# Attention scores and column sums as fp32r products of split operands, in the second block

## The reference

```python
h = rmsnorm(x, attn_norm[l])
sb_q, sb_k, sb_v, df_q, df_k, df_v = split(h @ w_in[l])        # 512 columns each
# stick-breaking attention, 8 heads of 64
z = q @ k.T * scale                                            # strict causal
w = exp(log_sigmoid(z) + sum of log_sigmoid(-z) over later keys)
sb_out = w @ v
# differential attention, 4 heads with 2 maps of 64, values of 128; q and k through rope
p = softmax(where(allowed, q @ k.T * scale, neg))              # for each map
df_out = rmsnorm((p[0] - lam * p[1]) @ v, subln_norm[l]) * (1 - lambda_init)
x = x + concat(sb_out, df_out) @ w_o[l]
h = rmsnorm(x, mlp_norm[l])
x = x + square(relu(h @ w_ff1[l])) @ w_ff2[l]                  # 4096 hidden
```

## Time and profile before

| | |
|---|---|
| median of 3 runs | 1955.8 us (1955.64 to 1956.62) |
| profiled execution, its own time | 1955.69 us |
| its span | 1953.9 us |
| mean granted TensorE clock | 0.999 of full |
| TensorE busy | 98% of the span |
| VectorE, ScalarE, GpSimd busy | 47%, 43%, 45% |

### The profile page before, as it was taken

One profiled execution on the slowest core, in us unless ns is written; L12 is line 12 of the kernel. 1 busy time (PEld: TensorE's weight loads), 2 busy tenths in 40 slices (PEclk: granted clock), 3 DMA queues, 4 the chain that ended last, 5 costly groups with the idle time before them and its releaser, 6 DMA issues. The chain is left out here.

```text
span 1953.9 us, 25592 instructions
## 1 busy us (share of the span) xinstructions
PE 1923.8 (98%) x9150; PEld 1510.5 (77%) x9150; DVE 916.7 (47%) x1420; ACT 834.5 (43%) x1269; POOL 881.6 (45%) x1188
## 2 busy tenths in 40 slices
PE   9999999999999999999999999999999999999998
PEld 7866766788888887777688888887777688888887
DVE  5487877432241346777541313133777643222132
ACT  4466555543242345555532223134555542222233
POOL 4322221456456465343355455454443355454543
PEclk9999999999999999999999999999999999999999
DMA  8211111233234233222134233333222223243322
GB/s 234 65 44 44 34 44 33 87 106 110 84 89 119 76 96 99 75 66 75 48 107 116 78 108 97 87 97 95 78 66 76 65 85 110 86 119 86 109 86 76
DMA packets 318100, 168.77 MB, mean 86 GB/s; under 512 B 15028, under 2 KB 313367, under 8 KB 317847
## 3 DMA queue, kind: packets, MB, share of 16 engines
q1 hardware_dynamic: 314432, 162.38, 28.9%
q10 hardware_dynamic: 3542, 4.76, 1.0%
HBM read 160.29 MB, written 2.10 MB: 83 GB/s over the span
## 5 line engine op out<-in xcount | busy, mean ns | idle before, releaser
L737 POOL TENSOR_TENSOR wlo<-raw,whi 128x256 fp32r<-128x256 f32 x1164 | 865.2, 775 | 1042.2 <-ACT whi L778 1042.2
L1621 PE MATMUL accs<-Xh,whi 128*128 128x512 f32 x1448 | 581.3, 401 | 0.1
L1623 PE MATMUL accs<-Xh,wlo 128*128 128x512 f32 x1448 | 565.1, 390 | 0.0
L1622 PE MATMUL accs<-Xl,whi 128*128 128x512 f32 x1448 | 563.9, 389 | 0.0
L778 ACT ACTIVATE whi<-raw 128x1024 fp32r<-128x1024 f32 x291 | 307.7, 1061 | 267.6 <-PE accs L1623 218.5
L1621 PEld LDWEIGHTS accs<-Xh,whi 128*128 128x128 f32 x1448 | 272.1, 188 | 58.6 <-issue 3.7
L1623 PEld LDWEIGHTS accs<-Xh,wlo 128*128 128x128 f32 x1448 | 271.8, 188 | 58.4
L1622 PEld LDWEIGHTS accs<-Xl,whi 128*128 128x128 f32 x1448 | 272.4, 188 | 56.1 <-issue 3.6
L1621 PE MATMUL accs<-Uh,whi 128*128 128x512 f32 x744 | 289.7, 389 | 0.8 <-DVE xT L1210 0.8
L1622 PE MATMUL accs<-Ul,whi 128*128 128x512 f32 x744 | 289.4, 389 | 0.0
L1623 PE MATMUL accs<-Uh,wlo 128*128 128x512 f32 x744 | 289.4, 389 | 0.0
(11 more groups left out here) (303 smaller groups left out, 1913.8 us busy)
## 6 DMA issues: line engine op xcount, KB each, us to landing
raw<-in_w_ff_dram SPq DMA_DIRECT2D x128, 512.0 KB
raw<-in_w_in_dram SPq DMA_DIRECT2D x71, 512.0 KB
raw<-in_w_gate_up_dram SPq DMA_DIRECT2D x44, 512.0 KB
raw<-in_w_down_dram SPq DMA_DIRECT2D x16, 512.0 KB
raw<-in_w_o_dram SPq DMA_DIRECT2D x16, 512.0 KB
px<-W ACTq DMA_DIRECT2D x64, 64.0 KB, 2.0
raw<-in_w_down_dram SPq DMA_DIRECT2D x8, 384.0 KB
W<-in_x_dram SPq DMA_DIRECT2D x4, 512.0 KB, 6.1
```

Source lines behind the costliest of these rows:

```text
L737: pool.tensor_tensor(lo[:, ks], raw[:, unit_no % RAW, ks], hi[:, ks].bitcast(F32), ALU.subtract).then_inc(sems["wlo"], 1)
L1621: mmul(y, whi[:, slot, k], xh[:, k], start=(i == 0), stop=False)
L1622: mmul(y, whi[:, slot, k], xl[:, k], start=False, stop=False)
L1623: last = mmul(y, wlo[:, slot, k], xh[:, k], start=False, stop=(i == len(ks) - 1))
```

## The change

Scores: the queries and keys of the second block get split as the weights do. ScalarE writes the rounded value into a free column tile of `Uh`, GpSimd the rest into `Ul`, at the items `sbq`, `sbk` and `rope`; for `rope` only with `j` < 3. The score product becomes three fp32r products for each head, for `qb` > 0. Column sums: `ssq` (new item `ssplit`, ScalarE and VectorE, at the end of the `prep` items) and the squares of `dv` (ScalarE squares `O` twice, GpSimd subtracts) are split too, and the sum is two fp32r products with a matrix of ones; the factor 1/1024 or 1/128 moves into ScalarE's logarithm. The order of the other items stays as it is.

```diff
+SB_Q, SB_K, DF_Q, DF_K = 3, 7, 2, 6
-    return s
+    return s + [("ssplit",)]                      # outputs(); also behind the last ffn_round of a layer
...
+                elif item[0] == "dv":             # GpSimd
+                    c = 4 + item[1]
+                    pool.wait_ge(sems["O_act"], at("O_act", 1))
+                    pool.tensor_tensor(Ul[:, c], sq[:, :], Uh[:, c].bitcast(F32), ALU.subtract).then_inc(sems["s_lo"], 1)
+                elif item[0] in ("sbq", "sbk", "rope"):
+                    split = qk_split(item)
+                    if split:
+                        src, c = split
+                        pool.wait_ge(sems["qk_hi"], at("qk_hi", 1))
+                        pool.tensor_tensor(Ul[:, c], src, Uh[:, c].bitcast(F32), ALU.subtract).then_inc(sems["qk_lo"], 1)
...
+                elif kind == "ssplit":            # ScalarE
+                    act.wait_ge(sems["sq"], at("sq"))
+                    act.wait_ge(sems["xl"], at("xl"))
+                    A(Uh[:, 0], ssq[:, :], ACT.Copy).then_inc(sems["s_hi"], 1)
...
+                    A(Uh[:, 4 + item[1]], O[:, :], ACT.Square).then_inc(sems["s_hi"], 1)    # dv, ahead of the square into sq
...
+                elif kind in ("sbq", "sbk"):
+                    src, c = qk_split(item)
+                    act.wait_ge(sems["acc"], at("acc", 1))
+                    A(Uh[:, c], src, ACT.Copy).then_inc(sems["qk_hi"], 1)
+                    act.wait_ge(sems["qk_hi"], at("qk_hi", 1))
+                elif kind == "rope" and qk_split(item):
+                    src, c = qk_split(item)
+                    act.wait_ge(sems["rp"], at("rp", 1))
+                    A(Uh[:, c], src, ACT.Copy).then_inc(sems["qk_hi"], 1)
+                    act.wait_ge(sems["qk_hi"], at("qk_hi", 1))
...
+                elif kind == "ssplit":            # VectorE
+                    dve.wait_ge(sems["s_hi"], at("s_hi", 1))
+                    TTn(Ul[:, 0], ssq[:, :], Uh[:, 0].bitcast(F32), ALU.subtract).then_inc(sems["s_lo"], 1)
...
+            def scores(bank, q, k, qb):           # TensorE
+                n = P * (qb + 1)
+                for a, b in ((Uh, Uh), (Ul, Uh), (Uh, Ul)):
+                    for h in range(2):
+                        mmul(bank[:, h, 0:n], a[hrows(h), q, P * qb:n], b[hrows(h), k, 0:n], start=(a is Uh and b is Uh), stop=False)
+            def column_sums(c):
+                pe.wait_ge(sems["ones_r"], 1)
+                pe.wait_ge(sems["s_lo"], at("s_lo"))
+                mmul(M[:, :], ones_r[:, :], Uh[:, c], start=True, stop=False)
+                return mmul(M[:, :], ones_r[:, :], Ul[:, c], start=False, stop=True)
...
-                    mmul(M[:, :], o1024, ssq[:, :], start=True, stop=True).then_inc(sems["M_fill"], 1)
+                    column_sums(0).then_inc(sems["M_fill"], 1)
...
-                    mmul(M[:, :], o128, sq[:, :], start=True, stop=True).then_inc(sems["M_fill"], 1)
+                    column_sums(4 + item[1]).then_inc(sems["M_fill"], 1)
...
-                    for h in range(2):
-                        mmul(S[:, h, 0:n], sbq[hrows(h), P * qb:n], sbk[hrows(h), 0:n], start=True, stop=False)
+                    if qb:
+                        pe.wait_ge(sems["qk_lo"], at("sb_split"))
+                        scores(S, SB_Q, SB_K, qb)
...
+                    if qb and item[1] < 3:        # d1
+                        pe.wait_ge(sems["qk_lo"], at("df_split"))
+                        scores(TT, DF_Q, DF_K, qb)
```

More of the change, by code:

```diff
@@ L133 @@
     "lay": dict(),
-    "sbq": dict(acc=1), "sbk": dict(acc=1),
+    "sbq": dict(acc=1, qk_hi=1, qk_lo=1), "sbk": dict(acc=1, qk_hi=1, qk_lo=1),
     "dfr": dict(acc=1, swap=1), "rope": dict(rp=1),
@@ L149, in events_of @@
         return dict(S_fill=1, S_act=1)
+    if kind == "rope" and item[2] < 3:
+        return dict(rp=1, qk_hi=1, qk_lo=1)
     if kind == "hn1" and item[1] == 3:
@@ L189, in marks_of @@
     if kind == "dv":
-        return dict(at_read="O_fill", o_sq="O_act")
+        return dict(at_read="O_fill")
     if kind == "on1":
@@ L398, in ffn_round @@
                 out.append(("prep", c, ("vec", R_AN + c)))
-        return out
+        return out + ([("ssplit",)] if last else [])
     s += [("rotary",)] + ffn_round(8, 0, False) + ffn_round(8, 1, False) + ffn_round(6, 2, True)
@@ L607, in build, with qk_split @@
         ssc, scb, scr = nsm[:, 0:8], nsm[:, 8:12], nsm[:, 12:16]
+        def qk_split(item):
+            if item[0] == "sbq":
+                return sbq, SB_Q
+            if item[0] == "sbk":
+                return sbk, SB_K
+            return ((dfk, DF_K) if item[1] else (dfq, DF_Q)) if item[2] < 3 else None
         def pt_view(at, qb):
@@ L1822, in stage @@
                     pe.wait_ge(sems["S_dve"], at("S_dve"))
-                    for h in range(2):
-                        mmul(S[:, h, 0:n], sbq[hrows(h), P * qb:n], sbk[hrows(h), 0:n], start=True, stop=False)
+                    if qb:
+                        pe.wait_ge(sems["qk_lo"], at("sb_split"))
+                        scores(S, SB_Q, SB_K, qb)
+                    else:
+                        for h in range(2):
+                            mmul(S[:, h, 0:n], sbq[hrows(h), P * qb:n], sbk[hrows(h), 0:n], start=True, stop=False)
                     for h in range(2):
@@ L1852, in stage @@
                     pe.wait_ge(sems["T_dve"], at("T_dve"))
-                    for m in range(2):
-                        mmul(TT[:, m, 0:n], dfq[hrows(m), P * qb:n], dfk[hrows(m), 0:n], start=True, stop=False)
+                    if qb and item[1] < 3:
+                        pe.wait_ge(sems["qk_lo"], at("df_split"))
+                        scores(TT, DF_Q, DF_K, qb)
+                    else:
+                        for m in range(2):
+                            mmul(TT[:, m, 0:n], dfq[hrows(m), P * qb:n], dfk[hrows(m), 0:n], start=True, stop=False)
                     for m in range(2):
```

38 lines of the change are left out of this document (27 added, 11 removed).

## The result

The changed kernel takes 2059.22 us (median, 2057.94 to 2059.82) against 1956.21 us (1955.64 to 1958.23) of the kernel before beside it: ratio 1.0524, 95% interval 1.0506 to 1.0542, 103.0 us slower. The forecast was slower, 2041 us, with a range of 2004 to 2065. The profiled execution took 2058.95 us (span 2057.1), the one before 1955.69 (span 1953.9).

A forecast was written before the change was run, and what follows sets the result against it. TensorE, busy 98% of the span, was taken as the bound. 1955.7 + 76.4 of waits - 6.7 of savings outside the stops = 2025.4; with 15.4 for the clock, 2041 us, range 2004 to 2065.

The forecast's parts named there:

- Rival 5: GpSimd is not held at its subtractions, so the products' 11.1 us are the whole result: 1944.6 us; chance 0.03.
- rival 1: TensorE's clock stays up or is back at once after the stops: 2025 us; chance 0.15.
- The forecast's 76.4: Delay from TensorE's new waits in both layers, 38.2 us each: 10.0 + 11.3 + 11.3 + 3.85 + 1.75.
- The second steady stop: Steady period, rope 1 ahead of the next mmA sq: TensorE stops for some 6.5 us.
- the first period: At j = 0, rope's subtractions delay TensorE: 5.0 us at the first stop, 10.0 us in all.
- The sign that I had named: TensorE's first product of mmA dv and mmA sq waits for GpSimd's wlo 4 to 7 us, three periods per layer.
- Rival 2: The second stop doesn't inherit the first; steady period costs 6.0 instead of 11.3 us: 2000, with some clock 2005; chance 0.09.
- rival 3: The two heads' fp32r score products don't overlap; each set costs +0.96 instead of -0.42 us: 2054 us; chance 0.05.
- rival 4: Each fp32r score round pays its weight load; the counted sets give +1.9 instead of -3.9 us: 2047 us; chance 0.05.
- 15.4 us forecast: Clock loss of TensorE behind its stops, taken as 1.1 us each; upper bound 2.8 each, 39 in all.
- the 14: Forecast stops of TensorE over both layers: four of 4.6, four of 5.0, two of 5.1, four of 6.5 us.
- the other insertions: Remaining inserted splits stay hidden in the steady period; at a layer's start they cost under 1 us, left to the range.

The follow-up runs named there:

- Experiment 1: The changed kernel with GpSimd's subtractions issued behind the quarters of the next two units (last dv of a layer: one): 1989.27 us, ratio 1.0170.
- experiment 8: Kernel 7 with all splits of queries and keys made, but the scores taken as float32 products: 1966.51 us, ratio 1.0050.
- experiment 2: The changed kernel with spare, unread products on TensorE in front of the places where it will stop: 2035.64 us, ratio 1.0406.
- Experiment 12: Kernel 7 with every GpSimd subtraction in the second block cut into four of 128 columns: 1956.59 us, ratio 1.0001.
- kernel 7: Kernel 6 with dv and on1 of each layer's last pair as in the kernel before: 1960.82 us, ratio 1.0022.
- 10: Kernel before plus only split column sums, dv's subtraction behind one unit, last pair as before, float32 scores: 1953.57 us, ratio 0.9987.
- kernel 9: Kernel before with only the five norms' column sums made as two fp32r products: 1955.10 us, ratio 0.9996.
- kernel 6: Kernel 5 with ScalarE's copy for rope moved behind the whi of the next mmA: 1964.96 us, ratio 1.0044.
- kernel 5: Kernel 1 with GpSimd's subtraction of dv behind the quarters of one unit instead of two: 1980.88 us, ratio 1.0123.

## Why the prediction was right, and where it was not

**The mechanism** was right: GpSimd and ScalarE walk the list in order, a subtraction that waits for a result of the moment takes away the lead of two units, and TensorE stops at `mmA dv`, at the next `mmA sq`, at the first early unit and at the last `on1`. Experiment 1 shows it directly: the same work in another place leaves no stop for quarters. Rival 5 (GpSimd not held) fell with GpSimd's waits of 133.9 and 106.8 us, rival 1 (the clock stays up) with the 16 low stretches.

**The stops** came to 68.2 us by the rows. The forecast's 76.4 is the delay that they cause, with what the items between them save already taken off: 68.2 less 4.3 (11 saved in all, 6.7 counted apart), so 63.9, is to be laid beside it. The chain from the rotated result to the two quarters measured 853.49 - 850.00 = 3.49 us against 3.75, since the subtraction took 1.27 us where I took 1.5. The second steady stop was 6.30 against 6.5. The first was 3.43 against 4.6: the result was there at 833.04, as TensorE finished the masks, and not 0.9 us behind, since TensorE was itself late by small waits. In the first period the stops were 4.23 and 3.41 us where I had 10.0 in all; in the last, 4.70 (forecast 5.1) and 2.10 (2.15). The sign that I had named, waits of 4 to 7 us for quarters in three periods, came as 3.3 to 6.3.

```profile
774.93 0.80 PE L1691 MATMUL accs<-Xh,whi 128*128 128x512 f32 x1 [4.23 <-POOL wlo L751]
...
979.73 0.47 PE L1716 MATMUL accs<-Uh,whi 128*128 128x512 f32 x1 [4.70 <-issue]
```

**Rival 2** (the second stop doesn't inherit the first) is refuted: ScalarE's swap DMAs went out behind `dv`'s squares at 844.61, VectorE's multiplication followed 3.97 us later (forecast 3.93), and the time is 54 us above that rival's 2005.

**The products** were nearly right: 5.2 us for the scores by the rows of their items against 5.9, a set 0.37 where I took 0.42, and a sum 0.36 to 0.45 cheaper against 0.40. That experiment 8 came to 5.7 is in part luck, since the clock has a share in it. Rivals 3 (heads don't overlap) and 4 (each round pays its load) are refuted too: by rival 3 a set would have cost 0.96 more, and the rule behind rival 4 isn't borne out, since rounds on the same rows follow each other 0.22 us apart.

**The clock** was the term that was mis-sized: 15.4 us forecast, 35 by the rows and some 24 by experiment 2. I took 1.1 us for each stop, because "the stops are not so long that each must meet a fall"; but each of the changed kernel's did, also the two of 2.1 us at the last `on1`, which I had not counted among the 14. TensorE worked at the low level for 3.2 to 6.8 us behind each, of which half is lost: 2.2 us for each of 16 stretches. The upper bound that I had set, 39, was nearer. The Trainium skill (TensorE: Matmul & The Clock Gate, "HAM oscillation") has a kernel that loses the clock in every wait between two bursts of products; the changed kernel's trace agrees, with 16 of 16. Other kernels here don't: see the last section.

**Not foreseen** were the small waits: 7.1 us of scores and 5.5 us of transposes waiting for VectorE. I had put "under 1 us" on the other insertions. Experiment 12 shows a reason for the wait at `d3` in kernel 7: GpSimd's longer instruction holds VectorE's. In the changed kernel itself no such instruction lies beside `d2` in these six places; there both operations of `d2` fall beside quarters (0.72 and 0.71 us, before 0.72 and 0.35), which is less than half of the 0.9 us that each transpose waits. The rest of it, and the waits of the scores, no run explains. What kept kernel 7 above before are the scores' splits: in its order they cost about 12 us (8 against 10), some 2 of it by the clock, about twice what their products save.

So 2041 missed 2059 by 18 us: 12.5 too many for the stops, 19.6 too few for the clock, 9.3 for small waits that had no term (77.5 - 68.2), and 1.7 that the rows don't place. That the miss is no larger is in part luck: the errors have opposite signs.

**Open.** All changed kernels, the one with only the norms' sums included, reach the end of the first units 0.6 us later than before and the end of the 17th to 28th 0.9 us later, in a stretch where the change adds only one copy of 0.23 us on VectorE, for the matrix of ones (at 69.8 us in kernel 9). The step at the 17th is a longer wait of TensorE for VectorE's scaling of the values (1.05 us at 163.7 in kernel 9, 0.73 before). It takes nearly half of the 2.0 us that the norms' sums save, and no run tells why. What the scores' splits cost beyond the 4 us that kernel 12 gave back was not taken apart further.

## What to carry to other kernels

Where engines walk one list in order, a new instruction costs by what is queued behind it: place it behind the work that feeds others, on each engine of its chain (GpSimd, then ScalarE here: 70 us and 16 us without taking away any work). Before an engine with idle time gets the work of a busy one, look at what it makes ahead of time, and at whose instructions it will hold. A stop of TensorE can be dearer than its length: allow for a half-speed stretch behind it, here 35 us on 68.

## What the runs showed of the hardware

- In the changed kernel a stop of TensorE of 2.10 us (1005.50 to 1007.60) had a granted clock of 0.50 behind it, while the stop of 1.1 us and those of 1.0 to 1.4 us in kernel 7 left it at full.

```profile
1005.60:1007.50 1.90, 0.00 (x0) 0.00 (x0) 0.00 (x0) 0.52 (x1) 1.31 (x2) 1.00 0.00 0
1007.60:1011.00 3.40, 3.40 (x8) 2.73 (x9) 0.67 (x1) 1.32 (x2) 2.62 (x4) 0.50 0.02 5
```

- The length of the stop alone doesn't decide it. Both stops of 2.10 us in kernel 6 (the first is shown there), one of 2.10 (at 971.1) in kernel 1 and one of 2.75 us (at 778.3) in kernel 5 left the clock at 1.00; one of 1.82 in kernel 8 and one of 1.37 us in kernel 12 had 0.50 behind them. Executions of one kernel differ in it too: of kernel 5's four, two took 1978.4 and 1978.6 us at a mean clock of 0.998, two 1983.2 and 1983.4 at 0.995. What else decides it isn't shown. Kernel 12, the stop and the stretch behind it:

```profile
1538.50:1539.80 1.30, 0.00 (x0) 0.00 (x0) 0.47 (x1) 1.18 (x5) 1.30 (x3) 1.00 0.00 0
1539.90:1543.30 3.40, 3.40 (x11) 2.37 (x12) 1.73 (x4) 1.03 (x4) 3.40 (x6) 0.50 0.17 48
```

- In the changed kernel's window of the 2.10 us stop the clock is still 1.00; in the stop of 6.3 us it fell before TensorE went on (mean 0.77).
- The first VectorE operation of `d2` at 128x128 took 0.29 us with no GpSimd instruction beside it (986.67 in the changed kernel), 0.72 beside a quarter and 1.25 to 1.26 beside the 128x512 subtraction; the second 0.35, 0.71 and 1.25. The other way round, `dv`'s subtraction took 2.10 us in kernel 7 against 1.28 in the changed kernel.
